# First-layer expert blocks in one run, gates multiplied in place from PSUM, key-2 one-hots on GpSimd

## The chip, the cores and the metric

The kernel runs on one core of a Trainium2 chip. The metric is the device time of one execution in microseconds (us), as the median of several runs. The engines are called PE (TensorE, matmuls; PEld is its weight load), DVE (VectorE), ACT (ScalarE), POOL (GpSimd) and SP (SyncE, which here only issues DMAs).

## The reference

Two transformer blocks over 256 tokens of width 1024, in float32. The change touches only the last layer of the second block, a product-key expert layer (PEER) with 16,384 experts:

```python
def peer_ffn(x, wq, keys, u_tab, v_tab):
    q = (xt @ wq).reshape(t, PEER_HEADS, 2, HALF_Q)            # 8 heads
    scores = jnp.einsum('thpd,hpnd->thpn', q, keys)            # 2 x 128 keys per head
    s_top, i_top = lax.top_k(scores, PEER_TOPK)                # 16 best of each half
    cand = (s_top[:, :, 0, :, None] + s_top[:, :, 1, None, :]).reshape(t, PEER_HEADS, 256)
    c_score, c_idx = lax.top_k(cand, PEER_TOPK)                # 16 best pairs
    expert = i1 * N_KEYS + i2                                  # i1, i2 from c_idx
    gates = jax.nn.softmax(c_score, axis=-1)
    ...
    u = jnp.take(u_tab, eb, axis=0)
    a = jax.nn.gelu(jnp.einsum('td,thkd->thk', xb, u), approximate=False)
    w = (gb * a).astype(xb.dtype)
    vv = jnp.take(v_tab, eb, axis=0)
    return jnp.einsum('thk,thkd->td', w, vv)
```

Then the residual is added and a last rmsnorm is taken.

## The kernel before

**The weight stream.** All weights come from one array `stream` of 128x1024 blocks (512 KB), in the order in which they are used, through a ring of four slots in SBUF. For each block SP issues the load (L303), ACT writes a rounded copy `w_high` (`split`, L471), DVE writes the remainder `w_low` (L866), and PE uses both. A product is three matmuls, high by high, low by high and high by low (`product`, L1383 to L1387).

**The expert layer is computed densely.** It does not gather experts. All 16,384 rows of `u_tab` are multiplied: 128 first-layer blocks of 128 experts each, block n being key 1 = n, with the 128 values of key 2 on the partitions. A first-layer block (`u_block`, L1747) is 24 matmuls of 256 columns into a PSUM bank, then a Gelu on ACT. The result is weighted by the gate of each expert and token, which is zero for nearly all, and split into `expert_w_high` (ACT, L824) and `expert_w_low` (DVE, L1356). A second-layer block (`v_block`, L1814) is 12 matmuls of 512 columns that accumulate into four PSUM banks. There are 128 of these too.

**The key search** runs on DVE, with POOL's help: `best16` finds the 16 best of each row, `keys_of` (L1289) reads out key 1 and key 2, and L1316 makes one-hots that POOL multiplies (L424). Between its steps DVE does the `w_low` of first-layer blocks, one per five short instructions or after a long one (`tick`, L1266).

**The order of the layer**, by constants `EARLY = 64`, `SEARCH = 60`, `TURN = 12`:

1. During the search PE computes the first 60 first-layer blocks (`early_tile`). ACT's Gelu writes one of four 128x256 buffers `gelu_out` (L783), and SP stores each to a DRAM array `early_gelu` (L314), as a buffer is needed again four blocks later.
2. The table of keys and gates is transposed by PE (L1788) and copied by ACT into `routeT` (L797).
3. The gate stage makes the full gate array `gates` of 128 x (128 x 256), 128 KB per partition, in 64 groups of four tokens. For a token, the outer product of a one-hot at key 2 and a row with the gate at key 1 is summed over the 128 (head, choice) rows, one fp32 matmul of 128x128 (L1800). Per group DVE compares a 512-column `iota` with key 1 and with key 2 (L1340, twice), POOL multiplies the key-1 one-hots by the gates (L433), PE does four matmuls, ACT copies them out of PSUM (L805). Four more first-layer blocks lie between the sixteens of groups (`early_tile` at L1757).
4. Sixteen turns of 12 blocks: four remaining first-layer blocks, four second-layer blocks for stored results (SP reads them back, L325), four for the new ones. POOL multiplies `gelu_out` by `gates` (L440), in 128 instructions of 128x256.

The gate stage's waits are: POOL waits for DVE's key-1 one-hots, PE for POOL's product and for ACT's copy of the group two before, DVE for PE's group two before.

Of the kernel before, what the change touches and what calls it, by code (L numbers as in the profile page):

```python
# [14 lines left out]
P = 128  # L15
# [17 lines left out]
    ("w_out_2", 8), ("peer_q", 16), ("peer", 256),  # L33
# [21 lines left out]
EARLY = 64  # L55
SEARCH = 60
TURN = 12
TURNS = EARLY // 4
EARLY_OUT = [SEARCH // 4 + (EARLY - SEARCH) // 2] * 2 + [SEARCH // 4] * 2
GROUPS = SEQ // 4 // (EARLY - SEARCH)  # L60
# [32 lines left out]
def build(nc, stream, w_dt, cols, small_row, rows, x, mem, keys, early, out):  # L93
# [133 lines left out]
    def by_head(t, k):  # L227
# [61 lines left out]
    def _(sp):  # L289
# [15 lines left out]
        b = BASE["peer"]  # L305
        with sp.Fori(0, (b + 8) // SLOTS - 1) as i:
            for n in range(SLOTS, 2 * SLOTS):
                load(n, i * SLOTS)

        with sp.Fori(0, SEARCH // SLOTS) as i:  # L310
            for n in range(SLOTS):
                load(b + 8 + n, i * SLOTS)
                sp.wait_ge(gelu_ok, i * SLOTS + (n + 1))
                sp.dma_start(early[bass.ds(i * SLOTS + n, 1)].rearrange("a p t -> (a p) t"), GE[:, n, :]  # L314
                             ).then_inc(early_out[n], 16)
        for n in range(SEARCH, EARLY):
            load(b + 8 + n)
            sp.wait_ge(gelu_ok, n + 1)
            sp.dma_start(early[n], GE[:, n % 2, :]).then_inc(early_out[n % 2], 16)

        def load_early(turn, k, dyn=None):

            n = 4 * turn + k
            src = early[n] if dyn is None else early[bass.ds(dyn * 4 + n, 1)].rearrange("a p t -> (a p) t")
            sp.dma_start(GE[:, k, :], src).then_inc(early_in[k], 16)  # L325


        for n in range(4):
            sp.wait_ge(early_out[n], 16 * EARLY_OUT[n])
        sp.wait_ge(g_sb, 64)  # L330
        for k in range(4):
            load_early(0, k)
        with sp.Fori(0, TURNS - 1) as i:
            for j in range(TURN):
                load(b + EARLY + 8 + j, i * TURN)
                if 5 <= j < 9:
                    sp.wait_ge(wt_low, i * 8 + j)
                    load_early(1, j - 5, i)
        for n in range(N_BLOCKS - 4, N_BLOCKS):
            load(n)  # L340
        for tt in range(TT):
            sp.wait_ge(final_ok, tt + 1)
            sp.dma_start(out[tt * P:(tt + 1) * P, :], TMP[:, tt, :]).then_inc(out_done, 16)
# [4 lines left out]
    def _(pool):  # L348
# [86 lines left out]
        def product(v, k, tile, dyn=None):  # L435

            g = GATES[:, tile, :] if dyn is None else GATES[:, bass.ds(dyn * 4 + tile, 1), :]
            if dyn is not None:
                g = g.rearrange("p a t -> p (a t)")
            pool.tensor_tensor(GE[:, k, :], GE[:, k, :], g, ALU.mult).then_inc(prod_ok, 1)  # L440

        pool.wait_ge(g_sb, 64)
        for k in range(4):
            pool.wait_ge(early_in[k], 16)
            product(k, k, k)
        with pool.Fori(0, TURNS - 1) as i:
            for k in range(4):
                pool.wait_ge(gelu_ok, i * 4 + (EARLY + k + 1))
                product(4 + k, k, EARLY + k, i)
            for k in range(4):  # L450
                pool.wait_ge(early_in[k], i * 16 + 32)
                product(8 + k, k, 4 + k, i)
        for k in range(4):
            pool.wait_ge(gelu_ok, 2 * EARLY - 4 + k + 1)
            product(2 * EARLY - 4 + k, k, 2 * EARLY - 4 + k)
        pool.wait_ge(prod_ok, 2 * EARLY)
        pool.dma_start(ROWG[:], rows[4].partition_broadcast(P)).then_inc(row_in, 16)
# [3 lines left out]
    def _(act):  # L461
# [314 lines left out]
        b = BASE["peer"]  # L776

        def early_tile(n, buf, written, dyn=None):

            act.wait_ge(w_used, at(b + n + 1, dyn, 4))  # L780
            if dyn is not None or written:
                act.wait_ge(early_out[buf], at(16 * written, dyn, 16))
            act.activation(GE[:, buf, :], PS[:, n % 2 * 512:n % 2 * 512 + SEQ], ACT.Gelu).then_inc(gelu_ok, 1)  # L783
            split(b + n + 4, 1, None if dyn is None else dyn * 4)

        for n in range(4):
            early_tile(n, n, 0)
        with act.Fori(1, SEARCH // 4) as i:
            for n in range(4):
                early_tile(n, n, 0, i)  # L790
# [4 lines left out]
        def route_copy(tt):  # L795
# [1116 lines left out]
```

## Time and profile before

| | us |
|---|---|
| median of 3 runs (2004.01 to 2009.28) | 2004.1 |
| the profiled execution: span of its trace | 2004.9 |
| PE busy | 1785.5 (89%) |
| DVE busy | 1164.9 (58%) |
| ACT busy | 880.5 (44%) |
| POOL busy | 246.4 (12%) |

The span is the time from the first to the last instruction of one profiled execution, and it stands 0.8 us above the median. The profile has no other time of that execution. Busy shares are averages over stages with different limits, so the stage in question is read by itself below. PE's busy time is modelled from issue times and is no measure of its peak.

### The profile page before, as it was taken

How to read it: one execution, taken by the hardware profiler on the slowest of the kernel's cores; microseconds unless marked ns; L12 is line 12 of the kernel's file. 1: busy time of each engine (PE TensorE's matmuls, PEld its weight loads, DVE VectorE, ACT ScalarE, POOL GpSimd, SP SyncE). 2: the span in 40 equal slices, each digit the busy share in tenths (PEclk: the TensorE clock that was granted, in tenths of full speed). 3: DMA queues.
4: the chain of work that ended last, by engine and by line, in shares of the span. 5: the costliest groups of instructions: out<-in, count | busy, mean ns of one | idle time of the engine just before them, and what ended most of it. 6: DMA issues, size and time to landing. Idle time of an engine off the chain costs nothing.

```text
span 2004.9 us, 30328 instructions
## 1 busy us (share of the span) xinstructions
PE 1785.5 (89%) x10352; PEld 1572.2 (78%) x10352; DVE 1164.9 (58%) x1627; ACT 880.5 (44%) x1259; POOL 246.4 (12%) x235
## 2 busy tenths in 40 slices
PE   5999899896687799979879998956789999999998
PEld 4887898775477688769859898955678888888887
DVE  4554545663454455456644599988765555555554
ACT  5443444533443444346333443423244444444444
POOL 0000000002000000000000001145532212121211
PEclk8999999987698899989889999979799999999999
DMA  5555453221152355444434466620045656565654
GB/s 190 185 184 168 164 183 125 87 104 42 48 172 85 115 189 181 163 138 165 129 105 139 146 212 201 191 66 26 13 156 198 212 198 212 198 210 201 207 201 144
DMA packets 97230, 303.58 MB, mean 151 GB/s; under 512 B 10896, under 2 KB 27536, under 8 KB 97040
## 3 DMA queue, kind: packets, MB, share of 16 engines
q1 hardware_dynamic: 96304, 299.06, 45.1%
q0 software_dynamic: 864, 3.67, 0.5%
q8 instruction: 42, 0.69, 0.1%
q14 instruction: 20, 0.16, 0.0%
HBM read 293.25 MB, written 9.44 MB: 151 GB/s over the span
## 4 chain that ended last, share of the span: by engine, by line
PE 76%; DVE 15%; ACT 4%; issue 2%; POOL 2%; DMA 0%; POOLq 0%; DVEq 0%; SPq 0%; ACTq 0%
PE ps L1385 23%; PE ps L1386 23%; PE ps L1387 23%; DVE w_low L866 3%; PE ps L1800 2%; POOL gate_at_key L433 2%; DVE gate_at_key L1340 2%; DVE xT_low L903 1%; DVE digit_hot L1316 1%; PE ps L1626 1%; ACT w_high L471 1%; PE ps L1521 1%; ACT xn L494 1%; PE ps L1449 0%; PE ps L1766 0%
## 5 line engine op out<-in xcount | busy, mean ns | idle before, releaser
L866 DVE TENSOR_TENSOR w_low<-ring,w_high 128x1024 fp32r<-128x1024 f32 x532 | 665.2, 1255 | 578.6 <-ACT w_high L471 578.2
L471 ACT ACTIVATE w_high<-ring 128x1024 fp32r<-128x1024 f32 x532 | 558.7, 1053 | 426.2 <-PE ps L1387 426.0
L1385 PE MATMUL ps<-xT_high,w_high 128*128 128x256 f32 x1600 | 462.9, 289 | 26.7 <-DVE xT_low L903 15.2
L1386 PE MATMUL ps<-xT_high,w_low 128*128 128x256 f32 x1600 | 459.9, 287 | 0.0
L1387 PE MATMUL ps<-xT_low,w_high 128*128 128x256 f32 x1600 | 459.6, 287 | 0.0
L1385 PEld LDWEIGHTS ps<-xT_high,w_high 128*128 128x128 f32 x1600 | 315.2, 197 | 30.7 <-DVE xT_low L903 16.4
L1386 PEld LDWEIGHTS ps<-xT_high,w_low 128*128 128x128 f32 x1600 | 315.1, 197 | 0.6
L1387 PEld LDWEIGHTS ps<-xT_low,w_high 128*128 128x128 f32 x1600 | 314.5, 197 | 0.0
L1385 PE MATMUL ps<-w_high,xT_high 128*128 128x512 f32 x480 | 192.3, 401 | 10.3 <-DVE memT_low L903 4.9
L1385 PE MATMUL ps<-w_high,expert_w_high 128*128 128x512 f32 x512 | 199.4, 389 | 0.0
L1386 PE MATMUL ps<-w_high,expert_w_low 128*128 128x512 f32 x512 | 199.4, 389 | 0.0
L1387 PE MATMUL ps<-w_low,expert_w_high 128*128 128x512 f32 x512 | 199.2, 389 | 0.0
L1386 PE MATMUL ps<-w_high,xT_low 128*128 128x512 f32 x480 | 189.5, 395 | 0.0
L1387 PE MATMUL ps<-w_low,xT_high 128*128 128x512 f32 x480 | 189.4, 395 | 0.0
L440 POOL TENSOR_TENSOR gelu_out<-gelu_out,gates 128x256 f32<-128x256 f32 x128 | 113.5, 888 | 401.3 <-DMA gelu_out<-early_gelu 247.5
L824 ACT ACTIVATE expert_w_high<-gelu_out 128x256 fp32r<-128x256 f32 x128 | 53.5, 418 | 175.7 <-PE ps L1387 127.8
L1800 PE MATMUL ps<-gate_at_key,one_at_key 128*128 128x128 f32 x512 | 86.5, 322 | 42.9 <-POOL gate_at_key L433 42.4
L1800 PEld LDWEIGHTS ps<-gate_at_key,one_at_key 128*128 128x128 f32 x512 | 74.1, 223 | 54.7 <-ACT gates L805 40.5
L1385 PE MATMUL ps<-w_high,hT_high 128*128 128x512 f32 x272 | 109.2, 401 | 7.1 <-DVE hT_low L903 2.9
L1385 PEld LDWEIGHTS ps<-w_high,xT_high 128*128 128x128 f32 x480 | 91.9, 191 | 30.0 <-DVE memT_low L903 5.3
L1387 PEld LDWEIGHTS ps<-w_low,expert_w_high 128*128 128x128 f32 x512 | 96.1, 188 | 20.2
L1385 PEld LDWEIGHTS ps<-w_high,expert_w_high 128*128 128x128 f32 x512 | 96.2, 188 | 19.5
(327 smaller groups left out, 2154.7 us busy)
## 6 DMA issues: line engine op xcount, KB each, us to landing
ring<-in_stream SPq DMA_DIRECT2D x532, 512.0 KB, 3.3
early_gelu<-gelu_out SPq DMA_DIRECT2D x64, 128.0 KB, 3.7
gelu_out<-early_gelu SPq DMA_DIRECT2D x64, 128.0 KB, 3.1
row_gain<-in_rows POOLq DMA_DIRECT2D x5, 512.0 KB, 4.3
h<-in_x SPq DMA_DIRECT2D x1, 1024.0 KB, 5.1
mem_sb<-in_mem SPq DMA_DIRECT2D x1, 1024.0 KB, 9.6
keys_sb<-in_keys POOLq DMA_DIRECT2D x1, 1024.0 KB, 5.3
out<-tmp SPq DMA_DIRECT2D x2, 512.0 KB, 2.6
```

The costliest lines, as they stand in the source:

```text
L433: pool.tensor_tensor(hot, hot, gate, ALU.mult).then_inc(hot4_ok, 1)
L440: pool.tensor_tensor(GE[:, k, :], GE[:, k, :], g, ALU.mult).then_inc(prod_ok, 1)
L471: act.activation(WH[:, n % SLOTS, :], RING[:, n % SLOTS, :], ACT.Copy).then_inc(w_high, 1)
L494: act.activation(XN[:, tt, g * w:g * w + w], src[:, tt, g * w:g * w + w], ACT.Square, accum_out=STAT[:, n:n + 1]).then_inc(sq_done, 1)
L824: act.activation(WTH[:, v % 4, :], GE[:, v % 4, :], ACT.Copy).then_inc(wt_high, 1)
L866: dve.tensor_tensor(WL[:, n % SLOTS, :], RING[:, n % SLOTS, :], WH[:, n % SLOTS, :].bitcast(F32), ALU.subtract).then_inc(w_split, 1)
L903: dve.scalar_tensor_tensor(low[:, k0 + kt, :], XT_PS[:, kt, :], COLS[:, GAIN_COL[gain] + kt:GAIN_COL[gain] + kt + 1], high[:, k0 + kt, :]. ...
L1340: dve.tensor_tensor(hot[:, q:q + 4, :], IOTA[:].unsqueeze(1).to_broadcast([P, 4, P]), ROUTE_T[:, p, t].unsqueeze(2).to_broadcast([P, 4, P] ...
L1385: pe.matmul(out, high, w_hi, start=start, stop=False, skip_group_check=True)
L1386: pe.matmul(out, low, w_hi, start=False, stop=False, skip_group_check=True)
L1387: return pe.matmul(out, high, w_lo, start=False, stop=stop, skip_group_check=True)
L1800: last = pe.matmul(PS[:, o:o + P], OB[:, 4 * q + j, :], OA[:, 4 * q + j, :], start=True, stop=True)
```

## The change

- Stream order: all 128 first-layer blocks (`peer_u`), then all 128 second-layer blocks (`peer_v`).
- `expert_w` is a new array of 128 x (128 x 256) that takes the place of `gates`. Each Gelu writes its own slot of it. The stores to DRAM and the loads back are gone. The slots lie over the search's arrays, so ACT waits for `tops_ok` before slot 64, for the exponentials at 72, `route_ok` before slot 80, and the transposed table is copied after slot 95.
- DVE does 72 of the `w_low` up to the end of the search and then the other 56 in a loop. The gate stage starts when all 128 first-layer blocks are done.
- In the gate stage POOL makes the key-2 one-hots, four `tensor_scalar` of 128x128 per group, and DVE makes key-1 one-hots already multiplied by the gate, four `tensor_scalar` with two scalar operands per group. For each pair of groups DVE multiplies 1024 gates straight from PSUM into `expert_w` in place (`weigh`). ACT's copies, POOL's products and the array `gates` are gone. PE has four PSUM banks for the groups.
- The second-layer blocks then run in one loop, each with `expert_w_high` (ACT) and `expert_w_low` (DVE).
- The last gain row is loaded into an array of its own, and the output is written from another array.

```diff
-    ("w_out_2", 8), ("peer_q", 16), ("peer", 256),
+    ("w_out_2", 8), ("peer_q", 16), ("peer_u", 128), ("peer_v", 128),
...
+EXPS_AT, ROUTED_AT, ROUTE_T_AT = 72, 80, 96
+SCORES_FREE_AT = 64
+GROUP = 4
...
POOL
-        with pool.Fori(0, SEQ // 8) as i:
-            for q in range(2):
-                pool.wait_ge(key1_ok, i * 2 + (q + 1))
-                hot = OA[:, 4 * q:4 * q + 4, :]
-                gate = ROUTE_T[:, 2, bass.ds(i * 8 + 4 * q, 4)].unsqueeze(2).to_broadcast([P, 4, P])
-                pool.tensor_tensor(hot, hot, gate, ALU.mult).then_inc(hot4_ok, 1)
...
-            pool.tensor_tensor(GE[:, k, :], GE[:, k, :], g, ALU.mult).then_inc(prod_ok, 1)
...
+        pool.wait_ge(rt_ok, 2)
+        for group in range(GROUPS):
+            if group >= 2:
+                pool.wait_ge(g_ps, group - 1)
+            for j in range(GROUP):
+                t = GROUP * group + j
+                last = pool.tensor_scalar(OB[:, group % 2, j, :], IOTA[:], ROUTE_T[:, 1, t:t + 1], None, ALU.is_equal)
+            last.then_inc(key2_ok, 1)
...
ACT
+        u_tiles(0, SCORES_FREE_AT)
+        act.wait_ge(tops_ok, 2)
+        u_tiles(SCORES_FREE_AT, EXPS_AT)
...
+        act.wait_ge(prod_ok, GROUPS // 2)
+        for v in range(4):
+            high(v)
+        with act.Fori(0, (EXPERT_BLOCKS - 4) // 4) as i:
+            for v in range(4):
+                act.wait_ge(w_used, i * 4 + (m + v + 1))
+                high(v + 4, i * 4)
+                split(m + v + 4, 1, i * 4)
...
DVE
-        split(b + PB + ticks[1], SEARCH - 2 - ticks[1])
-        ticks[1] = SEARCH - 2
         keys_of(1)
+        split(b + PB + ticks[1], EXPS_AT - ticks[1])
...
+        with dve.Fori(0, (EXPERT_BLOCKS - EXPS_AT) // 4) as i:
+            split(b + PB + EXPS_AT, 4, i * 4)
...
+        def key1_gate(group, dyn=None, late=True):
...
+            for j in range(GROUP):
+                k1, gate = (ROUTE_T[:, a, bass.ds(at(GROUP * group + j, dyn, 4 * GROUP), 1)] for a in (0, 2))
+                last = dve.tensor_scalar(OA[:, group % 2, j, :], IOTA[:], k1, gate, ALU.is_equal, ALU.mult)
+            last.then_inc(key1_ok, 1)
+        def weigh(pair, dyn=None):
+            dve.wait_ge(g_ps, at(2 * pair + 2, dyn, 4))
+            w = GE[:, :, bass.ds(at(2 * GROUP * pair, dyn, 4 * GROUP), 2 * GROUP)]
+            o = pair % 2 * 1024
+            dve.tensor_tensor(w, PS[:, o:o + 1024].rearrange("p (t n) -> p n t", n=P), w, ALU.mult).then_inc(prod_ok, 1)
...
PE
+            if late:
+                pe.wait_ge(prod_ok, at(group // 2 - 1, dyn, 2))
+            for j in range(GROUP):
+                o = 512 * (group % 4) + j * P
+                last = pe.matmul(PS[:, o:o + P], OB[:, group % 2, j, :], OA[:, group % 2, j, :], start=True, stop=True)
...
+        pe.wait_ge(gelu_ok, EXPERT_BLOCKS)
```

**DVE's queue in the gate stage**, the body of the loop. Before, two groups per turn of the loop; `gate_at_key` is the array of key-1 one-hots, `one_at_key` that of key-2 one-hots, `ISA` a register instruction of the sequencer:

```order
L1340 ISA [waits gates_psum]
L1340 TENSOR_TENSOR gate_at_key_114<-iota,routeT 128x512
L1340 ISA
L1340 TENSOR_TENSOR one_at_key_115<-iota,routeT 128x512
L1337 REGISTER_ALU
L1340 ISA [waits gates_psum]
L1340 TENSOR_TENSOR gate_at_key_114<-iota,routeT 128x512
```

In the changed kernel, the second group of a pair and the product:

```order
L1254 ISA [waits gates_psum]
L1254 TENSOR_SCALAR gate_at_key_112<-iota,routeT 128x128
L1254 ISA
L1254 TENSOR_SCALAR gate_at_key_112<-iota,routeT 128x128
L1254 ISA
L1254 TENSOR_SCALAR gate_at_key_112<-iota,routeT 128x128
L1254 ISA
L1254 TENSOR_SCALAR gate_at_key_112<-iota,routeT 128x128
L1262 ISA [waits gates_psum]
L1262 TENSOR_TENSOR expert_w<-ps,expert_w 128x128x8
```

Two long comparisons per group have become four short ones with a register instruction ahead of each, and every second group is followed by the product of the pair before, which waits for PE's matmuls of that pair.

**POOL's queue in the gate stage.** Before, in a loop:

```order
L433 ISA [waits ones_at_key1]
L433 TENSOR_TENSOR gate_at_key_114<-gate_at_key_114,routeT 128x512
L430 REGISTER_ALU
L433 ISA [waits ones_at_key1]
L433 TENSOR_TENSOR gate_at_key_114<-gate_at_key_114,routeT 128x512
```

In the changed kernel, written out for all 64 groups:

```order
L403 TENSOR_SCALAR one_at_key_113<-iota,routeT 128x128 [waits gates_psum]
L403 TENSOR_SCALAR one_at_key_113<-iota,routeT 128x128 x3
L403 TENSOR_SCALAR one_at_key_113<-iota,routeT 128x128 [waits gates_psum]
L403 TENSOR_SCALAR one_at_key_113<-iota,routeT 128x128 x3
L403 TENSOR_SCALAR one_at_key_113<-iota,routeT 128x128 [waits gates_psum]
```

POOL no longer stands behind DVE: it waits only for PE to have used the group two before.

**DVE at the end of the search.** Before:

```order
L866 TENSOR_TENSOR w_low<-ring,w_high 128x1024 [waits w_high_done] x2
L1293 TENSOR_REDUCE route<-digit_hot 128x128 [waits hot_ok]
L866 TENSOR_TENSOR w_low<-ring,w_high 128x1024 [waits w_high_done]
L1293 TENSOR_REDUCE route<-digit_hot 128x128
L866 TENSOR_TENSOR w_low<-ring,w_high 128x1024 [waits w_high_done]
L1329 TENSOR_REDUCE gate_sum<-cand_top 128x8 [waits gate_exp]
```

In the changed kernel:

```order
L1205 TENSOR_REDUCE route<-digit_hot 128x128 [waits hot_ok]
L778 TENSOR_TENSOR w_low<-ring,w_high 128x1024 [waits w_high_done]
L1205 TENSOR_REDUCE route<-digit_hot 128x128
L778 TENSOR_TENSOR w_low<-ring,w_high 128x1024 [waits w_high_done] x15
L1240 TENSOR_REDUCE gate_sum<-cand_top 128x8 [waits gate_exp]
```

The reduction moves ahead of two `w_low`, and 15 of them stand where one stood, ahead of the last softmax steps.

## Rows read from the trace of the kernel before

**Rows 1.** The page: busy time of each engine; chain of waits by engine.
```profile
PE 1785.5 (89%) x10352; PEld 1572.2 (78%) x10352; DVE 1164.9 (58%) x1627; ACT 880.5 (44%) x1259; POOL 246.4 (12%) x235
...
PE 76%; DVE 15%; ACT 4%; issue 2%; POOL 2%; DMA 0%; POOLq 0%; DVEq 0%; SPq 0%; ACTq 0%
```

**Rows 2.** Busy time in four stretches; columns as in its first row.
```profile
core 0: us, PE busy (x) PEld busy (x) DVE busy (x) ACT busy (x) POOL busy (x), PEclk, DMA share, GB/s
1126.00:1307.40 181.40, 171.68 (x1392) 171.02 (x1392) 171.04 (x455) 78.22 (x118) 22.03 (x4) 0.97 0.68 203
1307.40:1321.80 14.40, 1.54 (x8) 1.02 (x7) 10.55 (x13) 3.61 (x6) 0.00 (x0) 0.61 0.57 182
1321.80:1465.20 143.40, 99.51 (x610) 87.46 (x608) 113.93 (x132) 44.86 (x74) 84.01 (x64) 0.87 0.04 14
1465.20:1997.80 532.60, 532.59 (x3071) 472.43 (x3072) 296.75 (x316) 258.31 (x382) 114.13 (x129) 1.00 0.60 199
```

**Rows 3.** Timeline, 1291 to 1322: start, length, engine, line, what; in brackets idle and releaser.
```profile
1291.66 2.29 DVE L1316 TENSOR_TENSOR digit_hot<-cand_digits_f,iota 128x2048 f32<-128x2048 f32 x1
...
1295.00 6.73 DVE L1316 TENSOR_TENSOR digit_hot<-cand_digits_f,iota 128x2048 f32<-128x2048 f32 x1
...
1301.81 5.48 POOL L424 TENSOR_TENSOR digit_hot<-digit_hot,top_at_f 128x2048 f32<-128x2048 f32 x1 [2.23 <-DVE digit_hot L1316]
1302.79 4.53 DVE L1321 COPY gate_sum<-cand_top 128x8 f32<-128x8 f32 x1
...
1309.83 2.28 DVE L1293 TENSOR_REDUCE route<-digit_hot 128x128 f32<-128x2048 f32 x1
...
1312.03 1.22 DVE L866 TENSOR_TENSOR w_low<-ring,w_high 128x1024 fp32r<-128x1024 f32 x1
...
1320.68 0.49 ACT L797 ACTIVATE routeT<-ps 128x384 f32<-128x384 f32 x1 [9.95 <-DMA early_gelu<-gelu_out]
...
1321.31 0.87 PE L1788 MATMUL ps<-ident,route 128*128 128x128 f32 x3 [3.03 <-ACT routeT L797]
```

**Rows 4.** Timeline of PE: first matmul of eight second-layer blocks, four first-layer blocks, next.
```profile
1643.32 0.40 PE L1385 MATMUL ps<-w_high,expert_w_high 128*128 128x512 f32 x1
...
1665.11 0.28 PE L1385 MATMUL ps<-xT_high,w_high 128*128 128x256 f32 x1
...
1676.62 0.40 PE L1385 MATMUL ps<-w_high,expert_w_high 128*128 128x512 f32 x1
```

**Rows 5.** Timeline, the gate stage: a slow group's matmuls, then one group of four tokens.
```profile
1347.76 1.87 PE L1800 MATMUL ps<-gate_at_key,one_at_key 128*128 128x128 f32 x8 [0.81 <-POOL gate_at_key L433]
...
1400.08 1.15 DVE L1340 TENSOR_TENSOR gate_at_key<-iota,routeT 128x512 f32<-128x512 f32 x1 [0.30 <-PE ps L1800]
...
1400.81 1.15 PE L1800 MATMUL ps<-gate_at_key,one_at_key 128*128 128x128 f32 x8 [0.89 <-POOL gate_at_key L433]
...
1401.42 1.31 POOL L433 TENSOR_TENSOR gate_at_key<-gate_at_key,routeT 128x512 f32<-128x512 f32 x1 [0.74 <-DVE gate_at_key L1340]
...
1402.11 1.17 DVE L1340 TENSOR_TENSOR gate_at_key<-iota,routeT 128x512 f32<-128x512 f32 x1 [0.28 <-PE ps L1800]
```

**Rows 6.** Groups by line and form: shapes nearest to the new instructions, and ACT's.
```profile
L896 DVE TENSOR_SCALAR xn<-h,stat 128x1024 f32<-128x1024 f32 x6 | 4.6, 768 | 1.6 <-ACT stat L507 1.6
...
L1112 DVE TENSOR_TENSOR ssd_out<-ssd_out,ps 128x1024 f32<-128x1024 f32 x2 | 2.4, 1220 | 17.9 <-PE ps L1631 10.7 <-PE ps L1626 7.2
...
L471 ACT ACTIVATE w_high<-ring 128x1024 fp32r<-128x1024 f32 x532 | 558.7, 1053 | 426.2 <-PE ps L1387 426.0 <-DMA ring<-in_stream 0.2
L824 ACT ACTIVATE expert_w_high<-gelu_out 128x256 fp32r<-128x256 f32 x128 | 53.5, 418 | 175.7 <-PE ps L1387 127.8 <-POOL gelu_out L440 47.9
```

**Rows 7.** Timeline, 892 and 916: DVE TENSOR_SCALAR beside a short GpSimd instruction, and alone.
```profile
891.96 0.84 DVE L896 TENSOR_SCALAR xn<-h,stat 128x1024 f32<-128x1024 f32 x1 [0.27 <-ACT stat L507]
891.97 0.29 POOL L402 COPY in_chunk<-upto 128x128 f32<-128x128 f32 x1
...
916.51 1.38 DVE L1171 TENSOR_SCALAR forget<-forget,lower_bound 128x256 f32<-128x256 f32 x4 [1.67 <-ACT forget L722]
```

More of the change, by code:

```diff
@@ L90, in at, with build @@
     return static if dyn is None else dyn * scale + static
-def build(nc, stream, w_dt, cols, small_row, rows, x, mem, keys, early, out):
+def build(nc, stream, w_dt, cols, small_row, rows, x, mem, keys, out):
     ctx = ExitStack()
@@ L303, in load @@
             sp.dma_start(RING[:, n % SLOTS, :], src).then_inc(loaded[n % SLOTS], 16)
-        b = BASE["peer"]
-        with sp.Fori(0, (b + 8) // SLOTS - 1) as i:
+        with sp.Fori(0, N_BLOCKS // SLOTS - 1) as i:
             for n in range(SLOTS, 2 * SLOTS):
                 load(n, i * SLOTS)
[L310 to L340, printed above, removed]
         for tt in range(TT):
             sp.wait_ge(final_ok, tt + 1)
-            sp.dma_start(out[tt * P:(tt + 1) * P, :], TMP[:, tt, :]).then_inc(out_done, 16)
+            sp.dma_start(out[tt * P:(tt + 1) * P, :], RESULT[:, tt, :]).then_inc(out_done, 16)
         sp.wait_ge(out_done, 32)
@@ L425, in _ @@
                                    ALU.mult).then_inc(hot_ok, 1)
[L428 to L457 removed]
+        pool.wait_ge(rt_ok, 2)
[6 more added lines that the diff above has]
+            last.then_inc(key2_ok, 1)
+        pool.dma_start(LAST_GAIN[:], rows[4].partition_broadcast(P)).then_inc(row_in, 16)
     @block.scalar
@@ L775, in _, with u_tile, u_tiles @@
         act.wait_ge(injected, 1)
[L776 to L790, printed above, removed]
+        b, m = BASE["peer_u"], BASE["peer_v"]
+        def u_tile(n, dyn=None):
+            act.wait_ge(w_used, at(b + n + 1, dyn))
+            slot = GE[:, n, :] if dyn is None else GE[:, bass.ds(dyn + n, 1), :].rearrange("p a t -> p (a t)")
+            act.activation(slot, PS[:, n % 2 * 512:n % 2 * 512 + SEQ], ACT.Gelu).then_inc(gelu_ok, 1)
+            split(b + n + 4, 1, dyn)
+        def u_tiles(n0, n1):
+            with act.Fori(0, (n1 - n0) // 4) as i:
+                for n in range(4):
+                    u_tile(n0 + n, i * 4)
+        u_tiles(0, SCORES_FREE_AT)
+        act.wait_ge(tops_ok, 2)
+        u_tiles(SCORES_FREE_AT, EXPS_AT)
         for tt in range(TT):
@@ L793, in _ @@
             act.activation(CTOP[:, tt, :, :], CTOP[:, tt, :, :], ACT.Exp).then_inc(gexp_ok, 1)
-        def route_copy(tt):
+        u_tiles(EXPS_AT, ROUTED_AT)
+        act.wait_ge(route_ok, 2)
+        u_tiles(ROUTED_AT, ROUTE_T_AT)
+        for tt in range(TT):
             act.wait_ge(rt_ps, tt + 1)
@@ L845, in _, with high @@
-        m, v = m + (TURNS - 1) * TURN, (TURNS - 1) * 8
-        for k in range(4):
-            act.wait_ge(w_used, m + k + 1)
-            act.wait_ge(wt_low, v + k + 1)
-            act.activation(GE[:, k, :], PS[:, k * 512:k * 512 + SEQ], ACT.Gelu).then_inc(gelu_ok, 1)
-            split(m + k + 4, 1)
+        u_tiles(ROUTE_T_AT, EXPERT_BLOCKS)
+        def high(v, dyn=None):
+            slot = GE[:, v, :] if dyn is None else GE[:, bass.ds(dyn + v, 1), :].rearrange("p a t -> p (a t)")
+            act.activation(WTH[:, v % 4, :], slot, ACT.Copy).then_inc(wt_high, 1)
@@ L1372, in _ @@
+        for v in range(4):
+            low(v)
+        with dve.Fori(0, (EXPERT_BLOCKS - 4) // 4) as i:
+            for v in range(4):
+                low(v + 4, i * 4)
+                split(m + v + 4, 1, i * 4)
         dve.wait_ge(row_in, 16 * 5)
@@ L1876 @@
     v = g["peer_v_2"].reshape(P, P, BLK)
-    turns = [part.reshape(TURNS, 4, P, BLK) for part in (u[EARLY:], v[:EARLY], v[EARLY:])]
     kv = panels(g["xa_wkv"])
```

245 lines of the change are left out of this document (85 added, 160 removed).

## The prediction

> **What bounds the kernel now.** I read the page's busy times and chain first: PE is busy 89% of the span and is 76% of the chain [rows 1]. Then I cut the span at the places where the expert layer changes character, with the busy time per stretch [rows 2]. Up to 1307.4 (PE's 60th first-layer block) PE is busy 171.7 of 181.4 us while DVE searches, so both are full. From 1307.4 to 1321.8 PE does 1.5 us of work in 14.4: it waits for the end of the search. From 1321.8 to 1465.2 is the gate stage, 143.4 us with four first-layer blocks in it, and there no engine is full: PE 99.5, DVE 113.9, POOL 84.0. From 1465.2 to 1997.8 PE is busy throughout, and what is left, 2004.9 - 1997.8 = 7.1 us, is the tail. So the change can gain in the two middle stretches, 157.8 us together, and nowhere else, since PE's number of matmuls stays the same.
>
> In the gate stage one group of four tokens takes 1402.11 - 1400.08 = 2.03 us, a round trip [rows 5]: DVE compares (its row is 1.15 long, and ends after POOL's), POOL multiplies for 1.31, PE's four matmuls take 1.15, then the next group. At the lower clock the matmuls take 1.87.
>
> **PE's unit prices.** Eight second-layer blocks take 1665.11 - 1643.32 = 21.79 us, 2.72 each, and four first-layer blocks take 1676.62 - 1665.11 = 11.51, 2.88 each [rows 4]. As a check, 64 x 2.88 + 128 x 2.72 = 532.5, the stretch as measured [rows 2].
>
> **Part 1: all first-layer blocks in one run.** After 1307.4 PE needs the `w_low` of block 60. In the changed order DVE first reads out the keys of the second token tile: the copy that started at 1302.79 and took 4.53 ends at 1307.3, and with the small subtraction behind it and a 2.28 reduction [rows 3] it reaches 1309.9. A `w_low` is 1.22 long, of which the next instruction hides some 0.1, so block 60 can start at 1311.1, and it ends at 1314.0. Behind it stands the second reduction, and block 61 starts at 1314.5. From then on DVE has one `w_low` of 1.22 per block [rows 3] and ACT a Gelu of 256 columns, near the 0.42 of its row of that width, and 1.05 for `w_high` [rows 6], against PE's 2.88, so PE is continuous: 67 blocks x 2.88 = 193.0, to 1507.5. Added: the transposes of the routing table now stand between blocks 95 and 96. ACT copies the first half only after the Gelu of block 95 and one `w_high` (about 1.5), copies for 0.49, and PE transposes for 0.87 [rows 3]; I take 3.0. Last Gelu and its wait: 0.5. End at 1511.0.
>
> The stores to DRAM and loads back go. They cost one visible wait, ACT's 9.95 us until the last store had landed [rows 3], but that wait ran beside DVE's reductions until 1317.4 and ended the stretch only by 3 us; it is within the 14.4. In the last stretch PE never waited for the loads, so their absence is worth nothing there. SP's load of 512 KB per 2.88 us is 182 GB/s, and 203 and 199 are moved now [rows 2].
>
> **Part 2: the gate stage.** Let p be the time of a pair of groups, 32 pairs. On DVE a pair is eight key-1 instructions and one product. Neither shape is in the trace. Four TENSOR_SCALAR of 256 columns with two scalar operands take 1.38 [rows 7]. With 1024 columns and one scalar operand one takes 0.77 [rows 6], so a column costs under 0.5 ns and 128 fewer save 0.06 each: 1.38 - 0.24 = 1.14 for four, 2.3 for eight. The product of 1024 columns with one input from PSUM is 1.22 [rows 6]; its stride is new, and I take no surcharge. That is 3.5, less the overlap of an instruction's end with the next one's start, so 3.3 to 3.5 if DVE never waits. PE has 2 x 1.15 = 2.3 per pair, up to 3.7 at the lower clock [rows 5]: hidden under DVE, except in part of the slow groups. POOL's eight instructions are nearest to its copy of 128 columns, 0.29 [rows 7], so 2.3 per pair; with a scalar operand perhaps 0.4 each, 3.2. Hidden too, if it can run beside DVE. The register instructions ahead of DVE's comparisons are behind running instructions, and hidden at 0.28 a piece or nearly.
>
> What is late next is the crossing of DVE and POOL. A two-input DVE instruction of 2.29 took 6.73 while POOL ran, and a copy of eight columns took 4.53 beside POOL's 5.48 [rows 3]: one waits for the other. But where a 0.29 copy of POOL's ran at the start of a DVE TENSOR_SCALAR of 0.77, the latter took 0.84 [rows 7]; only 0.07 was lost, as POOL worked through DVE's first part. So the bounds for eight crossings are 0 and 8 x 0.29 = 2.3 per pair. I take the side of the short rows, 0.3, since these instructions are short as well, and 0.1 to 0.2 for PE's slow groups. **p = 3.4 + 0.5 = 3.9**; the gate stage is 32 x 3.9 = 124.8, plus 1.5 for its first group and last product. The bounds are 3.3 (nothing waits) and 3.3 + 2.3 = 5.6.
>
> The Trainium skill, "SBUF — State Buffer", section "Who interferes with whom", speaks against this change: a DVE instruction in a two-port mode and a GpSimd instruction exclude each other, "for the whole instruction". By it every crossing costs the other's full length, and p would be near 5. The long rows agree with it, and the short row shows less. By the same section the product, with one SBUF input, is free of this; no run here shows that.
>
> **Part 3: second-layer blocks.** First `expert_w_high` and `expert_w_low` before PE can start: 0.42 on ACT [rows 6], about as much on DVE for the same width, and their waits, 1.1. Then 128 x 2.724 = 348.7. ACT has 0.42 + 1.05 and DVE about 0.42 + 1.22 per 2.72, as now. Tail 7.1: the same instructions.
>
> **Sum.** 1511.0 + 1.5 + 32 p + 1.1 + 348.7 + 7.1 = 1869.4 + 32 p. With p = 3.9 that is 1994.2, against 2004.9 for the profiled execution. It stands 0.8 above the median, which I leave out: 1994. Break-even with the median is p = 4.2. In the old way the gate stage without its four blocks was 143.4 - 11.5 = 131.9, that is 4.1 per pair. So the gain in p is 6 to 7 us, and part 1 gives the other 4: of the 14.4 us of waiting 3.7 + 0.5 stay, and 3.0 + 0.5 + 1.5 + 1.1 are new.
>
> **The rivals.**
>
> A, *nothing crosses*: DVE runs its queue without waits, p 3.3 to 3.6, 1975 to 1985. For it speaks the 0.84 row [rows 7] and that POOL is no longer in the round trip. Against it: 2.3 us or more of POOL's work must fit beside 2.3 of DVE's and a 1.2 product in each pair, and half of it becomes possible only when DVE is back at comparisons.
>
> B, *the one-hots exclude each other*, which ends slower. Place: the eight key-1 instructions of each pair. Price: up to 0.29 for each, minus what falls under the product; 8 x 0.25 minus 0.5, p = 3.4 + 1.5 = 4.9, 2026. It decides from p = 4.4 (2010) on, an average delay of 0.12 per DVE instruction. For it speak the 6.73 and 4.53 rows [rows 3]; a POOL instruction with a scalar operand that takes 0.4 would bring it about as well. Against it: the 0.84 row.
>
> C, *PE's clock*: the mean granted clock in the stage is 0.87 now [rows 2]. If more groups ran at 1.87 us, with 2 x 1.87 + waits = 4.1 to 4.3 for such a pair, p would near 4.2 and nothing would change: 2004. Against it: PE's share of busy time rises, from 1.15 in 2.03 to 2.3 in 3.9.
>
> D, *the change doesn't bring the blocks under the search*: the search itself gives PE no more room than now, since PE was busy 171.7 of 181.4 us in it. The 56 later blocks run behind it, on PE's time. This is in my sum already; if instead the wait at 1307 had gone wholly, 4 us more would be gained.
>
> **How the numbers follow.** Forecast (p 3.65 to 4.15, 1986 to 2002) 0.43; A 0.15; B (4.4 and more) 0.25; C or a mixture around 4.2 to 4.4 0.17. The range leaves out 1 in 10 on either side: below p = 3.3 there is nothing on DVE's rows, so 1975; above, most of B is taken in, to p = 4.9, 2026. About 0.3%, 6 us, is what a measurement can tell from no change: under 1998 is faster, over 2010 slower. 1998 is p = 4.02, so faster takes A and four fifths of the forecast, which thins out towards its ends: 0.50. Slower is B: 0.25. Same is the rest: 0.25.
>
> **What would show it.** Right: PE without a gap from 1314 to about 1507 except 3 us near 1415; a period of 3.9 us between DVE's products; key-1 rows of 0.35 with some near 0.5; ACT idle in the gate stage; no waits of PE in the last 349 us. B: key-1 rows of 0.6 and a period near 5. A: no key-1 row over 0.4. The prediction is wrong if the product takes much over 1.22, if four POOL instructions take over 1.7, or if PE waits for loads in the first-layer run.

## The result, and the profile after

The changed kernel takes 2025.07 us (median of four runs, 2023.46 to 2026.65) against 2004.88 us (also of four, 2004.01 to 2009.28) before: the ratio is 1.0097, with a 95% interval of 1.0082 to 1.0111. It is slower by 1%, where 1994 was forecast. Its profiled execution has a span of 2021.6 us.

The page: busy time of each engine, and the chain, as in [rows 1].

```profile
PE 1804.3 (89%) x10352; PEld 1588.8 (79%) x10352; DVE 1155.8 (57%) x1787; ACT 863.3 (43%) x1211; POOL 199.9 (10%) x299
...
PE 74%; DVE 13%; POOL 6%; ACT 4%; issue 2%; DMA 0%; ACTq 0%; DVEq 0%; SPq 0%
PE ps L1305 23%; PE ps L1307 23%; PE ps L1306 23%; POOL one_at_key L403 6%; DVE w_low L778 3%; PE ps L1719 1%; DVE xT_low L815 1%; DVE digit_hot L1228 1%; PE ps L1546 1%; ACT w_high L419 1%; PE ps L1441 1%; ACT xn L442 1%; PE ps L1369 0%; PE ps L1683 0%; DVE gate_sum L1233 0%
```

Busy time by stretch, cut where the stages of the changed kernel change; it answers to [rows 2].

```profile
core 0: us, PE busy (x) PEld busy (x) DVE busy (x) ACT busy (x) POOL busy (x), PEclk, DMA share, GB/s
1126.00:1307.00 181.00, 170.91 (x1376) 170.01 (x1374) 170.50 (x455) 94.69 (x130) 21.96 (x4) 0.96 0.49 163
1307.00:1420.00 113.00, 109.68 (x900) 109.45 (x901) 52.78 (x48) 55.34 (x83) 2.78 (x5) 0.98 0.56 186
1420.00:1511.00 91.00, 88.80 (x740) 88.59 (x739) 38.69 (x32) 42.24 (x64) 2.72 (x4) 1.00 0.52 177
1511.00:1664.00 153.00, 107.37 (x512) 93.48 (x512) 113.78 (x289) 0.00 (x0) 146.11 (x249) 0.70 0.02 8
1664.00:2021.00 357.00, 349.92 (x1536) 289.28 (x1536) 209.37 (x259) 174.74 (x259) 0.00 (x0) 0.99 0.53 179
```

POOL has less work than before over the whole span (199.9 us against 246.4), and is 6% of the chain against 2%. The fourth row says where: in the gate stage, 1511 to 1664, POOL is busy 146.1 of 153 us, and the first 3.8 of those 153 lie before its start at 1514.79, the last 3.1 behind its end. No other engine is full there. The first-layer blocks behind the search (second and third row) keep PE busy 198.5 of 204 us.

Timeline of the gate stage, columns as in [rows 3]: one pair of groups, from product to product.

```profile
1579.43 13.14 POOL L403 TENSOR_SCALAR one_at_key<-iota,routeT 128x128 f32<-128x128 f32 x22
1579.48 1.21 DVE L1262 TENSOR_TENSOR expert_w<-ps,expert_w 128x1024 f32 x1
...
1580.80 1.19 DVE L1254 TENSOR_SCALAR gate_at_key<-iota,routeT 128x128 f32<-128x128 f32 x4
1582.95 1.17 DVE L1254 TENSOR_SCALAR gate_at_key<-iota,routeT 128x128 f32<-128x128 f32 x4 [0.97 <-PE ps L1719]
...
1583.15 1.13 PE L1719 MATMUL ps<-gate_at_key,one_at_key 128*128 128x128 f32 x8 [0.38 <-issue]
1584.04 1.21 DVE L1262 TENSOR_TENSOR expert_w<-ps,expert_w 128x1024 f32 x1
```

POOL issues 22 comparisons end to end in 13.14 us, 0.60 each. DVE's rows have gaps released by PE. PE waits too, but the trace mostly doesn't name for what: of its idle time in the stage 30.0 us stand under "issue", 8.7 under POOL's one-hots and 7.1 under DVE's rows. That it is the one-hots follows from POOL, whose L403 has no gap but the two at its start, as its own view shows, and from the runs below in which POOL has less to do. The columns after the count are the shortest, median and longest instruction in ns.

```profile
L403 POOL TENSOR_SCALAR one_at_key<-iota,routeT x256: 596/605/1411, 1417.2 to 1660.3; 128x128 f32<-128x128 f32 x128
its engine sat idle before it (us, times) until:
  ACT routeT L749: 112.3, 1
  PE ps L1719: 92.1, 1
```

DVE's new instructions, by the same view:

```profile
L1254 DVE TENSOR_SCALAR gate_at_key<-iota,routeT x256: 332/345/484, 1511.4 to 1659.2; 128x128 f32<-128x128 f32 x128
its engine sat idle before it (us, times) until:
  PE ps L1719: 36.5, 43
...
L1262 DVE TENSOR_TENSOR expert_w<-ps,expert_w x32: 1209/1211/1225, 1517.5 to 1662.8; 128x1024 f32 x30, 128x1024 f32<-128x1024 f32 x2
```

The period of a pair is what lies between two products, (1662.8 - 1517.5) / 31 = 4.69 us. That is eight of POOL's instructions at 0.586, and not the 3.9 of the forecast.

### The profile page after: what moved, and what is told of

Read it like the earlier page. It is cut to its first block, busy times and chain, and to the rows that moved or that the text cites. A ratio compares the mean times of both kernels' runs of the same rounds, so it can differ in the third digit from the quotient of the medians.

```text
span 2021.6 us, 29989 instructions
## 1 busy us (share of the span) xinstructions
PE 1804.3 (89%) x10352; PEld 1588.8 (79%) x10352; DVE 1155.8 (57%) x1787; ACT 863.3 (43%) x1211; POOL 199.9 (10%) x299
## 4 chain that ended last, share of the span: by engine, by line
PE 74%; DVE 13%; POOL 6%; ACT 4%; issue 2%; DMA 0%; ACTq 0%; DVEq 0%; SPq 0%
PE ps L1305 23%; PE ps L1307 23%; PE ps L1306 23%; POOL one_at_key L403 6%; DVE w_low L778 3%; PE ps L1719 1%; DVE xT_low L815 1%; DVE digit_hot L1228 1%; PE ps L1546 1%; ACT w_high L419 1%; PE ps L1441 1%; ACT xn L442 1%; PE ps L1369 0%; PE ps L1683 0%; DVE gate_sum L1233 0%
## 5 line engine op out<-in xcount | busy, mean ns | idle before, releaser
L778 DVE TENSOR_TENSOR w_low<-ring,w_high 128x1024 fp32r<-128x1024 f32 x532 | 648.9, 1224 | 582.1 <-ACT w_high L419 581.7
L756 ACT ACTIVATE expert_w_high<-expert_w 128x256 fp32r (+1 forms) x128 | 53.2, 418 | 324.4 <-PE ps L1307 170.5
L403 POOL TENSOR_SCALAR one_at_key<-iota,routeT 128x128 f32<-128x128 f32 x256 | 151.0, 614 | 205.0 <-ACT routeT L749 112.3
L1719 PE MATMUL ps<-gate_at_key,one_at_key 128*128 128x128 f32 x512 | 107.4, 377 | 46.6 <-issue 30.0
L1719 PEld LDWEIGHTS ps<-gate_at_key,one_at_key 128*128 128x128 f32 x512 | 93.5, 274 | 60.4 <-issue 60.4
L730 ACT ACTIVATE expert_w<-ps 128x256 f32 x128 | 49.2, 384 | 162.6 <-PE ps L1307 162.4
```

Source lines behind the costliest of these rows:

```text
L403: last = pool.tensor_scalar(OB[:, group % 2, j, :], IOTA[:], ROUTE_T[:, 1, t:t + 1], None, ALU.is_equal)
L730: act.activation(slot, PS[:, n % 2 * 512:n % 2 * 512 + SEQ], ACT.Gelu).then_inc(gelu_ok, 1)
L756: act.activation(WTH[:, v % 4, :], slot, ACT.Copy).then_inc(wt_high, 1)
L778: dve.tensor_tensor(WL[:, n % SLOTS, :], RING[:, n % SLOTS, :], WH[:, n % SLOTS, :].bitcast(F32), ALU.subtract).then_inc(w_split, 1)
L1719: last = pe.matmul(PS[:, o:o + P], OB[:, group % 2, j, :], OA[:, group % 2, j, :], start=True, stop=True)
```

## The experiments

Each ratio is to runs of the kernel before on the same chip, whose median was 2006 to 2007 us. "Period" is again (start of the last product - start of the first) / 31.

**What POOL's instruction costs by itself.** The theory: the 0.60 us is the price of this form on POOL. The rival: it is a price of contention with DVE, as rival B of the forecast had it. 54 instructions were added near the start of the changed kernel, in runs of one form each:

```
+        pool.memset(PSRC[:], 1.0).then_inc(probe_ok, 1)
...
+        for o in range(0, 1024, 128):
+            pool.tensor_scalar(PROBE[:, o:o + P], UPTO[:], IDENT[:, 0:1], None, ALU.is_equal).then_inc(probe_ok, 1)
...
+        for o in range(0, 1024, 128):
+            pool.tensor_scalar(PROBE[:, o:o + P], UPTO[:], 1.0, None, ALU.is_equal).then_inc(probe_ok, 1)
...
```

> The changed kernel with 54 instructions added on GpSimd near the start, where VectorE hardly works: eight TENSOR_SCALAR of 128x128 each with pointer operand and is_equal, with an immediate and is_equal, with pointer and mult, with immediate and mult; three of 128x512 with pointer and is_equal, three with immediate and mult; eight TENSOR_TENSOR mult of 128x128; eight copies of 128x128. Their results are used by nothing. Theory T (the instruction itself is that slow): the first kind takes 0.60 us here too, as in the gate stage. Rival L (the port: a short instruction of about 0.3 us that waits for VectorE's): it takes 0.3 to 0.35 us here. If T holds, the other kinds say whether it is the pointer operand (immediates near 0.3), the comparison (mult near 0.3), or neither.

In order: comparison with a scalar from memory; with a constant; multiplication by a scalar from memory; by a constant; 512 columns with a scalar from memory; 512 with a constant; TENSOR_TENSOR; COPY.

```profile
L341 POOL TENSOR_SCALAR probe_out<-upto,ident x8: 592/593/612, 5.5 to 9.5; 128x128 f32<-128x128 f32 x8
...
L344 POOL TENSOR_SCALAR probe_out<-upto x8: 522/523/960, 10.2 to 14.1; 128x128 f32<-128x128 f32 x8
...
L347 POOL TENSOR_SCALAR probe_out<-upto,ident x8: 597/600/1328, 14.7 to 19.5; 128x128 f32<-128x128 f32 x8
...
L350 POOL TENSOR_SCALAR probe_out<-upto x8: 526/755/1261, 20.2 to 26.4; 128x128 f32<-128x128 f32 x8
...
L353 POOL TENSOR_SCALAR probe_out<-probe_src,ident x3: 1563/1563/1568, 27.0 to 30.1; 128x512 f32<-128x512 f32 x3
...
L356 POOL TENSOR_SCALAR probe_out<-probe_src x3: 1494/1495/1495, 31.7 to 34.7; 128x512 f32<-128x512 f32 x3
...
L359 POOL TENSOR_TENSOR probe_out<-upto,ones x8: 453/460/1441, 36.2 to 40.3; 128x128 f32<-128x128 f32 x8
...
L362 POOL COPY probe_out<-upto x8: 286/293/1298, 40.9 to 43.5; 128x128 f32<-128x128 f32 x8
```

Far from the gate stage the instruction takes 0.593 us; beside the first eight DVE has only two instructions, of 0.15 and 0.16 us. The operation makes no difference (0.593 against 0.600); the scalar from memory costs 0.07; and a column costs (1563 - 593) / 384 = 2.5 ns, which leaves about 0.27 fixed. A copy of the same width is half as long. So the instruction was underestimated by 1.5 to 2 times (0.29 to 0.4 each), and next to none of its 0.605 in the stage comes from the place. The fourth row's median of 0.755 is no price of its form: four of its eight took about 0.53, one 0.98 beside a DVE TENSOR_SCALAR of 128x1024 (0.76 us long), and three about 1.26 beside three `w_low` in a row. The probe was executed once, in 2026.9 us.

**Half of POOL's work.**

```
-            for j in range(GROUP):
+            for j in range(GROUP if group < 2 else 2):
```

> The changed kernel with half of GpSimd's one-hots left out: from the third group on, only the first two of four tokens get theirs, the others keep an old one, so their gates are those of other tokens. T: an instruction still takes 0.60 us, a group 1.2 us on GpSimd, 2.4 per pair, so VectorE's queue sets the period, 3.4 to 3.6 us per pair against 4.69, and the time falls by 32 x 1.1 to 1.3, to 1983 to 1990. L: the GpSimd instructions get shorter, as they meet fewer of VectorE's, and VectorE's key-1 rows too; the time falls as well, so the rows decide. If something else than GpSimd holds the stage (PE's clock, the round trip through PSUM), the period stays over 4 and the time over 2000.

The kernel leaves out the key-2 one-hots of two tokens in each group of four from the third group on. It takes 1984.38 us (1981.95 to 1986.59), ratio 0.9885 (0.9868 to 0.9902). POOL's instruction stays at 0.606 and the period falls to (1627.3 - 1525.6) / 31 = 3.28. With POOL out of the way the stage runs at DVE's pace, which the forecast had as 3.3 to 3.5, and the whole change would be a gain. The key-1 instructions are hardly shorter, 0.363 on the mean against 0.368, so what fell away is no delay of DVE by POOL but DVE's waiting for PE, 1.6 us in place of 36.5.

**A shorter form in the same place.**

```
-                last = pool.tensor_scalar(OB[:, group % 2, j, :], IOTA[:], ROUTE_T[:, 1, t:t + 1], None, ALU.is_equal)
+                last = pool.tensor_scalar(OB[:, group % 2, j, :], IOTA[:], 1.0, None, ALU.is_equal)
```

> The changed kernel with the key-2 comparison against a constant in the instruction in place of the key in memory (so the one-hots are those of key 1 for every token; this leaves out the routing by key 2, the amount of work is the same). The measured price of that form alone was 0.525 us against 0.595. Theory (GpSimd's queue, eight instructions a pair, is the bound): period 8 x 0.525 = 4.2 us instead of 4.7, time lower by 32 x 0.5 = 16 us, so 2007 to 2012 us. Rival (the bound is somewhere else and GpSimd only keeps busy beside it): 2022 us or more.

2007.48 us (2005.65 to 2013.21), ratio 1.0010 (0.9999 to 1.0021). POOL's median falls to 0.523 and the period to (1648.9 - 1522.1) / 31 = 4.09. Per instruction that is 0.511 against 0.586, so 0.075 less in each of 256 is 19 us, and the median fell by 17.6 (17.5 by the two ratios, which take out a difference between chips). POOL's queue sets the time of the stage, nearly one for one.

**The one-hots back on DVE**, in one instruction of 512 columns as before the change; POOL has nothing to do in the stage. This is the change without its third part.

```
+            t = bass.ds(at(GROUP * group, dyn, 4 * GROUP), GROUP)
+            dve.tensor_tensor(OB[:, group % 2, :, :], IOTA[:].unsqueeze(1).to_broadcast([P, GROUP, P]),
+                              ROUTE_T[:, 1, t].unsqueeze(2).to_broadcast([P, GROUP, P]), ALU.is_equal).then_inc(key2_ok, 1)
...
```

> The changed kernel with the key-2 one-hots on VectorE, one TENSOR_TENSOR is_equal of 128x512 per group as in the kernel before, and nothing on GpSimd in the gate stage. T: per pair eight key-1 instructions 2.3, two comparisons 2 x 0.6, the product 1.14: 4.6 us, about as now: 2020 to 2026, and key-1 rows of 0.345 as now. L: the same on VectorE, but if the key-1 rows were lengthened by GpSimd they would be shorter than 0.345 here.

2014.83 us (2012.79 to 2017.2), ratio 1.0044 (1.0027 to 1.0061), period (1651.9 - 1518.9) / 31 = 4.29. It is 5 to 11 us below what was expected, since DVE's instructions overlap more than I allowed: by their rows a pair is 8 x 0.342 + 2 x 0.686 + 1.22 = 5.3 us, and the comparisons are longer than the 0.6 expected. DVE idles 0.7 us in the whole stage. The key-1 rows answer the second question: 0.342 without POOL, 0.368 in the changed kernel. Two things follow. The first two parts alone don't pay: DVE is the bound then, at more than the 4.1 of the old way. And the move to POOL takes 1.0 off DVE's pair, from 4.29 to the 3.28 of the run with half of POOL's work, only to run into POOL's own 4.7.

**The one-hots on ScalarE**, which stands idle for 153.82 us of the changed kernel's gate stage. It makes max(0, 1 - (key - i)^2), four Squares and one Relu in place.

```
...
+            for j in range(GROUP):
+                last = act.activation(OB[:, group % 2, j, :], IOTA[:], ACT.Square, scale=-1.0, bias=ROUTE_T[:, 1, t:t + 1])
+            last.then_inc(ob_sq, 1)
+            act.wait_ge(ob_sq, group + 1)
+            act.activation(OB[:, group % 2, :, :], OB[:, group % 2, :, :], ACT.Relu, scale=-1.0, bias=1.0
+                           ).then_inc(key2_ok, 1)
```

> The changed kernel with the key-2 one-hots on ScalarE, which is idle in the gate stage: per group four ACTIVATE Square of (key 2 - iota), 128x128, and one Relu of (1 - that) over 128x512, exact for whole numbers; nothing on GpSimd. From rows of the kernel before, 0.29 for a Square of 128x128 and 0.58 for 512 columns, with overlaps 1.5 us per group, 3.0 per pair, under VectorE's 3.4 to 3.6. T: 1983 to 1992, faster than both kernels by over half a per cent. If the stage is held by PE's clock or the round trip: over 2000.

```profile
L757 ACT ACTIVATE one_at_key<-iota,routeT x256: 384/386/402, 1512.1 to 1629.4; 128x128 f32<-128x128 f32 x128
L760 ACT ACTIVATE one_at_key<-one_at_key x64: 629/630/632, 1513.4 to 1629.8; 128x512 f32<-128x512 f32 x64
```

1993.46 us (1990.92 to 1997.78), ratio 0.9941 (0.9924 to 0.9958). The period is (1631.7 - 1519.5) / 31 = 3.62, a little over DVE's own 3.3: ACT's queue has hardly a gap (0.8 us of waiting for PE in the whole stage), and is the bound by a small margin. The time is 1.5 us over the range expected. The reason is again a price from another row: a Square takes 0.386 and not 0.29, and a group 1.8 us of ACT's queue, not 1.5.

**What POOL beside DVE costs DVE.** The same kernel, with 192 of POOL's comparisons through the gate stage, written to spare memory that nobody reads.

```
+        for t in range(192):
+            pool.tensor_scalar(SPARE[:, t % GROUP, :], IOTA[:], ROUTE_T[:, 1, t:t + 1], None, ALU.is_equal
+                               ).then_inc(spare_ok, 1)
...
```

> As the run with the key-2 one-hots on ScalarE (period 3.62 us, 1993 us, eight key-1 instructions 2.22 us a pair), but GpSimd runs 192 of the same comparisons, 128x128, without pause through the gate stage into spare memory; nobody waits for them. Theory (sharing the port costs VectorE little): the key-1 instruction goes from 0.341 to 0.36 to 0.37 us, the product stays at 1.22, the period is 3.6 to 3.8 us, time 1993 to 2000 us. Rival (a lock for whole instructions): VectorE's 3.4 us per pair and GpSimd's 0.6 us instructions take turns, key-1 instructions take 0.6 us or more, period over 4.5 us, time over 2020 us.

DVE's key-1 instructions without POOL's (first row) and beside them (second row):

```profile
L1258 DVE TENSOR_SCALAR gate_at_key<-iota,routeT 128x128 f32<-128x128 f32 x256 | 71.0, 341 | 13.3 <-PE ps L1723 13.1
```

```profile
L1266 DVE TENSOR_SCALAR gate_at_key<-iota,routeT 128x128 f32<-128x128 f32 x256 | 76.0, 361 | 8.5 <-PE ps L1731 8.1
```

1992.38 us (1990.75 to 1993.36), ratio 0.9931 (0.9909 to 0.9953), with a period of (1631.7 - 1519.5) / 31 = 3.62: no change. DVE's instructions grow from a mean of 0.341 to 0.361 us, 0.16 a pair, and it idles less. ACT is the bound here and could hide that much, so the rows decide and not the time. The product stays at 1.21. Rival B's mechanism, in which each waits for the other's whole length, isn't there for these short instructions.

**Both producers.** Even groups stay on POOL (first piece) and odd ones go to ACT (second piece, with the Squares and the Relu of above), with a semaphore for each.

```
-        for group in range(GROUPS):
+        for group in range(0, GROUPS, 2):
...
+        for group in range(1, GROUPS, 2):
...
-            pe.wait_ge(key2_ok, at(group + 1, dyn, 4))
+            pe.wait_ge(key2_odd if group % 2 else key2_ok, at(group // 2 + 1, dyn, 2))
```

> The key-2 one-hots of the even groups stay on GpSimd (four comparisons at about 0.6 us, 2.4 us a pair), those of the odd groups go to ScalarE (four Squares and a Relu, 1.9 us a pair); nothing is left out. Theory (GpSimd's instruction is slow by itself and made it the bound): both lie under VectorE's queue, so the period of a pair falls from 4.7 us to VectorE's own 3.3 to 3.5, as with half the one-hots left out; time 1981 to 1990 us. Rival (VectorE and GpSimd hold the port against each other for whole instructions): with 2.4 us of GpSimd per pair added to VectorE's 3.4 the period would be 4.5 us or more, time 2015 us or more.

A miss: 1994.01 us (1993.29 to 1995.92), ratio 0.9939 (0.9922 to 0.9956), period (1632.8 - 1519.5) / 31 = 3.65, although POOL has half its work. The timeline shows why:

```profile
1580.51 2.33 POOL L405 TENSOR_SCALAR one_at_key<-iota,routeT 128x128 f32<-128x128 f32 x4 [1.31 <-PE ps L1731]
...
1582.97 2.05 PE L1731 MATMUL ps<-gate_at_key,one_at_key 128*128 128x128 f32 x16 [1.67 <-DVE gate_at_key L1266]
1584.22 2.33 POOL L405 TENSOR_SCALAR one_at_key<-iota,routeT 128x128 f32<-128x128 f32 x4 [1.39 <-PE ps L1731]
```

The two buffers alternate by group, so the even one belongs to POOL alone. POOL fills it in 2.33 us, PE reads it in half of 2.05, and only then may POOL start on the next: a ring of 1584.22 - 1580.51 = 3.71 us in which POOL idles 1.39. The middle row names DVE as what released PE, as DVE's key-1 rows ended 0.1 us after POOL's; over the whole stage the matmuls' waits stand under POOL's one-hots in 17 cases (25.5 us) and under DVE's rows in 14 (23.4 us). So the ring was an argument until the next run tested it.

**Both producers, four buffers.**

```
+    OB2 = sb("one_at_key2_more", [P, 2, GROUP, P], 60)
...
-            if group >= 2:
-                pool.wait_ge(g_ps, group - 1)
+            if group == 2:
+                pool.wait_ge(gelu_ok, EXPERT_BLOCKS)
+            if group >= 4:
+                pool.wait_ge(g_ps, group - 3)
...
```

> The split run again (even groups on GpSimd, odd ones on ScalarE; period 3.69 us, 1994.0 us), with four key-2 buffers where there were two, the new pair in the 8 KB at the end of the low half of x transposed, free from the last first-layer block on (4 KB of it are used). Nothing is left out. Theory: the split missed its 3.3 to 3.5 us because each producer had one buffer, so that GpSimd's 2.33 us and TensorE's read of that group, 1.05 us, followed each other in a ring (2.33 + 1.05 + 0.3 of semaphores = 3.7); with two buffers each the ring is off the path, the period is VectorE's 8 x 0.36 less overlap + 1.21 = 3.4 to 3.55 us, time 1984 to 1990 us. Rival (the split's 3.69 us come from VectorE beside GpSimd, or from TensorE): period still 3.65 to 3.7, time 1993 to 1995 us.

1982.10 us (1981.91 to 1982.66), ratio 0.9880 (0.9863 to 0.9898), 2 us under the range expected: it computes all of the kernel and beats both, before by 1.2% and the changed one by some 43 us. The period is (1623.5 - 1522.2) / 31 = 3.27. So neither POOL beside DVE nor PE had held the split at 3.65. The stretch of the gate stage, columns as in [rows 2], has DVE full, and POOL's ring is off the path.

```profile
1516.00:1625.00 109.00, 68.36 (x512) 62.96 (x512) 106.96 (x289) 59.89 (x157) 72.06 (x123) 0.97 0.03 10
```

DVE is busy 106.96 of 109 us and idles 1.6 for PE before its key-1 instructions, against 36.5 in the changed kernel.

## Why the prediction was wrong

- **End of the first-layer blocks.** Forecast 1511.0. DVE's stage begins at 1511.44 and PE's first gate matmul is at 1512.64, so the number is right, in part by luck. The search ended 2.3 us earlier than forecast (its copy ran from 1300.43 to 1304.95). Some of that went where 15 of the 24 matmuls of the first block behind it ran at the lower clock, 0.41 us long instead of 0.28, and the last first-layer matmul ended at 1508.80, where the forecast had 1510.5. Then DVE still had the `w_low` of the fourth second-layer block ahead of its gate stage (1510.29, 1.23 long), which the forecast had nowhere.
- **Loads and stores.** PE has no wait for loads in the last stretch. Right.
- **DVE's instructions.** Key-1 at 0.285 in the queue was the forecast (1.14 for four), the rows read 1.11 to 1.32 for four, and 2.13 for eight before POOL begins; the product 1.22, measured 1.21. Right. (The column price in that sum, under 0.5 ns, is (0.77 - 0.345) / 768 = 0.55 by the rows it names, which changes the four by 0.04.) Halving POOL's work and the run with four buffers put DVE's pair at 3.28 and 3.27, the low end of my 3.3 to 3.5.
- **POOL's instruction: the step that failed.** "POOL's eight instructions are nearest to its copy of 128 columns, 0.29 [rows 7], so 2.3 per pair; with a scalar operand perhaps 0.4 each, 3.2." They take 0.605, so eight take 4.7 in a row. They are not hidden under DVE's 3.4: the forecast let DVE's queue set the period, and POOL's sets it. The copy was a single instruction of another kind, and the 0.4 had no row at all. Two nearer rows were in the trace of before, in the view of POOL's instructions by name (shortest, median, longest in ns):

```profile
L440 POOL TENSOR_TENSOR gelu_out<-gelu_out,gates x128: 733/744/1811, 1469.9 to 1977.0; 128x256 f32<-128x256 f32 x128
```

```profile
L433 POOL TENSOR_TENSOR gate_at_key<-gate_at_key,routeT x64: 1299/1313/1320, 1323.6 to 1461.6; 128x512 f32<-128x512 f32 x64
```

  From 256 to 512 columns the time grows by (1313 - 744) / 256 = 2.2 ns a column, so 128 columns of that kind take 744 - 128 x 2.2 = 0.46 us, which is what the probe has for it. Eight of 0.46 are 3.7 a pair, more than DVE's 3.4: POOL as the bound could be read from before, though by the sum still at 1869.4 + 32 x 3.7 = 1988 us. That a TENSOR_SCALAR takes another 0.13 could not be read there.
- **The size of the miss.** The sum was 1869.4 + 32 p. The stage took 153.05 us, from 1511.0 to the end of the last product at 1664.05. With the measured period of 4.69, 32 pairs are 150.0, where the forecast had 124.8: 25.2 us by this one term. The first group and the last product took 3.0 instead of 1.5, which makes 26.7 of the 27.4 us between the sum's 1994.2 and the profiled span of 2021.6; the other terms hold in sum. The median, 2025.07, lies 3.5 above that span. The run that was profiled took 2023.46, so a time is some 1.9 us longer than its span, and the forecast set the two equal when it left out 0.8.
- **The range.** It reached from 1975 to 2026 and takes in the measured time only at its upper end, which came from rival B's price. B's mechanism is absent, so that is luck.
- **Crossings at the port.** 0.3 a pair was forecast. Key-1 instructions take 0.368 on the mean in the changed kernel and 0.341 with POOL silent, 8 x 0.027 = 0.22 a pair, and 0.16 by the run with POOL's spare work. Nearly right in size, and it costs nothing where DVE isn't the bound. Long instructions do delay each other: before the change DVE's 128x512 comparison with key 1 (L1340, both inputs in SBUF) began while POOL's product ran and took 1.07 us on the mean, the same comparison with key 2 took 0.68; and in the probe a POOL instruction of 0.53 took 0.98 beside a DVE TENSOR_SCALAR of 128x1024. Why the 128x128 comparisons are left nearly alone, and DVE's copy of eight columns in the forecast's rows (4.53) was not, no run shows. By the Trainium skill, "SBUF — State Buffer", section "Who interferes with whom", a DVE instruction in a two-port mode and a GpSimd instruction exclude each other for the whole instruction. If these comparisons are of that kind, which no row says, the rows disagree (0.341 became 0.361, not 0.6 or more). By the same section a DVE instruction with one SBUF input outside these modes is free of it. The product, whose other input is in PSUM, agrees: 1.217 alone and 1.210 beside POOL.
- **Rival B** gave 2026, near the result, but for another reason. It named a slower POOL instruction as a second way to the same end, with 0.4 as its size and DVE's waits as its mechanism. In the trace DVE hardly waits for a port; PE waits for one-hots. Its marks, key-1 rows of 0.6, are absent: the longest took 0.484. Of my own marks of failure, "if four POOL instructions take over 1.7" was the one that came true, with 2.4.
- **Rival C.** The granted clock in the gate stage is 0.70 in the changed kernel, with groups of eight records at 1.13 and others at 2.05, against 0.97 in the run with four buffers. It is low where PE waits most, behind POOL: a pair has the forecast's 2.3 us of matmuls at the higher clock, but in 4.7 us and not in 3.9. Since POOL never stops between 1514.79 and 1660.9, the low clock can have lengthened the stage only ahead of and behind that, by the first and the last groups' matmuls; whether it would in a kernel where POOL has some slack wasn't tried.
- **What the parts are worth.** The first two parts alone give +0.44% (the run with the one-hots on DVE), the third as written adds to that, and the same three parts with the one-hots spread over two engines and four buffers give -1.2%. The first part by itself wasn't run.

## What to carry to other kernels

Price an instruction that moves to another engine by a row of that engine and of the same kind, and where only another width is there, by its time per column. Then compare each engine's sum per loop turn, the helper's too: an engine that is busy 10% of the span, as POOL is in the changed kernel, can still be the bound of one stage. Where two engines share out the turns of a double buffer, each has a single buffer, and its fill and the consumer's read add up; give each two.

## What the runs showed that I had not expected

- GpSimd's TENSOR_SCALAR in f32 with a scalar in memory takes 2.5 ns a column and 0.27 us fixed, 0.593 for 128 columns and 1.563 for 512, comparison and product alike; its COPY of 128 columns takes 0.293 and its TENSOR_TENSOR 0.460. With a constant in place of the scalar in memory it takes 0.523. DVE's key-1 instruction of the same shape, with two operations, takes 0.341.
- ScalarE makes the one-hots of four tokens in 4 x 0.386 + 0.630 us by its rows, against GpSimd's 4 x 0.605; in their queues that is 1.8 us (3.62 / 2) against 2.3 (4.69 / 2).
- Shifts of some microseconds in stages that a kernel doesn't change are there between runs: the last `w_low` ahead of the gate stage starts at 1510.29 in the changed kernel and at 1514.87 in the run with four buffers. Periods within a stage tell the mechanism better than ends do.
